# Front pooling in two-tile jobs, one per step, with the turned rows copied by ScalarE

## The reference

```python
h = rms_norm(x, norm1_g) * (1 + scale1) + shift1
z = h @ w_in                      # 256 columns p for pooling, then q, k, v of 6 heads
def pool_mixer(p, w_pool, pool_scale):       # windows 2, 4, 8, 16 tokens, one for each 64 channels
    pooled = stack([centred_mean(p_i, w) - p_i for each window w])
    return einsum('btgc,gcd->btgd', pooled, w_pool) * pool_scale
mix = concatenate([pool, attn]) @ w_out
```

## Time and profile before

| | us |
|---|---|
| median of 3 runs | 3398.87 (3396.64 to 3400.84) |
| the profiled execution, its own time | 3397.15 |
| its span, first to last instruction | 3395.4 |
| TensorE busy in the span | 3183.7 |
| VectorE busy | 2274.7 |
| ScalarE busy | 1610.0 |
| GpSimd busy | 631.9 |
| mean granted TensorE clock, share of full speed | 0.976 |

### The profile page before, as it was taken

The page is one execution under the profiler, slowest core; times in us unless marked ns, Lnnn a source line. Parts: engine busy times, 40 slices in busy tenths (PEclk is TensorE's granted clock), DMA queues, the critical chain, the costliest instruction groups (busy, mean ns, idle before and its releaser), DMA issues. The chain is left out here.

```text
span 3395.4 us, 69378 instructions
## 1 busy us (share of the span) xinstructions
PE 3183.7 (94%) x23534; PEld 2970.9 (87%) x23534; DVE 2274.7 (67%) x3793; ACT 1610.0 (47%) x3529; POOL 631.9 (19%) x854
## 2 busy tenths in 40 slices
PE   6879999999999999998987993999999999999998
PEld 4869988988998898997775882999999999999998
DVE  4778877877887887777884446555555555555553
ACT  3436656666665665665552110444444444444442
POOL 2432233232223223221000000000010010000001
PEclk8989999999999999999998995999999999999999
DMA  8554334334334335333326551665666666566663
GB/s 281 200 184 143 111 122 141 116 116 150 112 113 151 114 116 158 111 112 100 102 71 229 191 187 62 209 187 184 186 185 195 194 195 191 186 186 186 186 186 101
DMA packets 373718, 530.68 MB, mean 156 GB/s; under 512 B 29530, under 2 KB 321626, under 8 KB 358362
## 3 DMA queue, kind: packets, MB, share of 16 engines
q1 hardware_dynamic: 363868, 494.52, 44.8%
q0 software_dynamic: 9728, 34.61, 4.5%
HBM read 439.10 MB, written 89.16 MB: 156 GB/s over the span
## 5 line engine op out<-in xcount | busy, mean ns | idle before, releaser
L2421 PE MATMUL ps_gu<-xT,e_w 128*128 128x272 f32 x6144 | 788.1, 290 | 3.6 <-DVE xT L2596 3.6
L2421 PEld LDWEIGHTS ps_gu<-xT,e_w 128*128 128x128 f32 x6144 | 778.6, 189 | 4.2 <-issue 4.0
L2585 DVE TENSOR_TENSOR e_w<-e_raw,e_w 128x2048 fp32r<-128x2048 f32 x192 | 440.0, 2291 | 419.1 <-ACT e_w L2493 409.4
L1054 ACT ACTIVATE e<-ps_s,negm 128x1024 f32<-128x1024 f32 (+2 forms) x416 | 473.6, 1146 | 249.3 <-DVE negm L1387 249.3
L1379 DVE TENSOR_REDUCE mx<-ps_s 128x1 f32<-128x1024 f32 (+3 forms) x428 | 520.5, 1232 | 68.0 <-PE ps_s L722 67.3
L722 PE MATMUL ps_s<-kT,qT 128*128 128x512 f32 (+1 forms) x1920 | 469.5, 384 | 12.4 <-ACT e L1054 11.9
L760 PE MATMUL ps_m<-v,aT 128*128 128x128 f32 x3456 | 471.2, 279 | 6.6 <-ACT aT L1040 3.8
L760 PEld LDWEIGHTS ps_m<-v,aT 128*128 128x128 f32 x3456 | 420.7, 191 | 34.8 <-issue 14.8
L722 PEld LDWEIGHTS ps_s<-kT,qT 128*128 128x128 f32 x1920 | 346.8, 190 | 83.4 <-ACT e L1054 15.2
L2440 PE MATMUL ps_gu<-hid,e_w 128*128 128x272 f32 x3072 | 412.3, 291 | 0.0
L790 PE MATMUL ps_m<-w,hT 128*128 128x384 f32 x2040 | 391.9, 340 | 3.9 <-DVE o L1435 3.9
(11 more groups left out here) (287 smaller groups left out, 3273.9 us busy)
## 6 DMA issues: line engine op xcount, KB each, us to landing
hT<-hT_d SPq DMA_DIRECT2D x85, 1024.0 KB, 5.3
e_raw<-w_gate SPq DMA_DIRECT2D x64, 1024.0 KB, 5.0
e_raw<-w_up SPq DMA_DIRECT2D x64, 1024.0 KB, 5.0
e_raw<-w_down SPq DMA_DIRECT2D x64, 1024.0 KB, 7.6
tab<-tabs_d SPq DMA_DIRECT2D x85, 256.0 KB, 2.7
hT_d<-hT SPq DMA_DIRECT2D x17, 1024.0 KB, 4.0
cat_o<-cat_d SPq DMA_DIRECT2D x17, 1024.0 KB, 6.2
w_lent<-w_ada SPq DMA_DIRECT2D x16, 1024.0 KB, 5.4
```

Source lines behind the costliest of these rows:

```text
L1054: nc.scalar.activation(out, src, ACT.Exp, bias=negm[:, s.par, c:c + 1], scale=HD ** -0.5, accum_out=acc).then_inc(exp_done.sem, 1)
L2421: mm = nc.tensor.matmul(ps_gu[:, 2 * (s % 2) + f, 0:SLOTS], w_view(s, a)[:, k, f * P:f * P + P], xT[:, b, k, :], start=(k == 0 and a + b = ...
L2585: nc.vector.tensor_tensor(w[:, s % RING, 1, :], raw[:, s % RAW, :], w[:, s % RING, 0, :].bitcast(F32), ALU.subtract).then_inc(w_lo, 1)
```

## The change

- Pooling jobs have two tiles and one half each: 16 jobs, and two for the prompt (`JOBS` = 18). From step 3 on, `pool_sums` of one job ends VectorE's step; its mix, high and low parts follow in the next step; its save is issued in the step after. Jobs 14 to 17 (`LATE` = 14) have `pool_sums` at the end of step 16 and in the first step of head 1, where the remaining mixes are.
- Early jobs take two pooled buffers, two halves of the space of `aT` and two halves of one PSUM bank in turn; late jobs have places of their own in the half of `kT` that head 1 fills later. The buffers pT, trig and junk move to other places, and window sums use two buffers, not three.
- The copies of turned q, k and pooling rows go from VectorE's step to ScalarE's next step, behind `squares_kq` and ahead of `high_rows`.
- `spread_prompt` runs twice each in steps 0 and 1.
- Waits for the saves are added in head 1: `copy_turned`, `copy_past`, and VectorE's `copy_kq`.

```diff
+    JOBS, LATE, SPAN = NS + 2, NS - 2, 2 * P + 2 * PAD
...
+cat_early = aT[:].rearrange("p a n -> p (a n)").rearrange("p (q t l n) -> p q t l n", q=2, t=2, l=2)
+late_at = kT_lent[:, 2 * KEYS:4 * KEYS]
+pooled_early = e_lent[:, 0:512].rearrange("p (q n) -> p q n", q=2)
...
 def mixed_at(n):
-    return ps_t[:, 1, :] if n >= 6 and n % 2 else ps_m[:]
+    nt = pool_job(n)[2]
+    return ps_m[:, 2 * P * (n % 2):2 * P * (n % 2) + nt * P]
...
@@ SP, first_pass(t), after save_q and ahead of save_rows @@
-        for n in jobs_of(t - 1):
-            save_pooled(n)
+        if t >= 5:
+            save_pooled(t - 5)
...
@@ SP, body, ahead of the loads @@
         if s.h == 1 and s.zero:
-            for n in range(6, 10):
+            for n in range(NT - 5, LATE + 2):
                 save_pooled(n)
...
@@ SP, body, after save_q @@
+        if s.h == 1 and s.zero:
+            for n in range(LATE + 2, JOBS):
+                save_pooled(n)
...
@@ TensorE, mix_pool @@
+        if n:
             pe.wait_ge(catp_hi, n)
             pe.wait_ge(catp_lo, n)
...
@@ TensorE, first_pass, between turn_rows and project_pool @@
-        if 1 <= s.i <= 4:
-            spread_prompt(s.i - 1)
-        for n in jobs_of(s.i):
-            mix_pool(n)
+        if s.i < 2:
+            spread_prompt(2 * s.i)
+        if s.i >= 4:
+            mix_pool(s.i - 4)
...
@@ after project @@
+        if s.i < 2:
+            spread_prompt(2 * s.i + 1)
+        if s.i == NS:
+            mix_pool(LATE - 1)
...
@@ TensorE, body: mix_pool(LATE) ahead of scores(s, 0); ahead of scores(s, 1): @@
         if s.h == 1 and s.zero:
-            for n in (8, 9):
+            for n in range(LATE + 1, JOBS):
                 mix_pool(n)
-            pe.wait_ge(catp_hi, 10)
-            pe.wait_ge(catp_lo, 10)
...
@@ ScalarE @@
     def high_pooled(n):
-        if n == 9:
-            act.wait_ge(cat_b_saved, 16)
-        elif n and not in_cat_b(n):
-            act.wait_ge(cat_a_saved, 16 * cat_a_uses(n))
+        if 2 <= n < LATE:
+            act.wait_ge(pool_saved[n % 2], 16 * (n // 2))
...
+    def copy_kq(s):
+        kq_ready.wait(act, s, 1)
+        qT_saved[s.par].wait(act, s)
+        nc.scalar.copy(qT_out[:, s.par, :], ps_t[:, 1, 0:2 * P]).then_inc(kq_copied.sem, 1)
+        nc.scalar.copy(kT[:, 0, :, PAST + P * (s.i - 1):PAST + P * s.i],
+                       ps_t[:, 1, 2 * P:4 * P].rearrange("p (c n) -> p c n", c=2)).then_inc(kq_copied.sem, 1)
...
@@ ScalarE, first_pass, between squares_kq and high_rows @@
+        if s.i:
+            copy_turned_rows(previous(s))
...
@@ then, ahead of copy_pool @@
+        if s.i >= 4:
+            high_pooled(s.i - 4)
...
@@ ScalarE, body: copy_turned_rows first, high_pooled(LATE) ahead of split_rest(1), after exps(s, 0): @@
+        if s.h == 1 and s.zero:
+            for n in range(LATE + 1, JOBS):
+                high_pooled(n)
...
@@ VectorE, first_pass, from means to its end @@
-        for n in jobs_of(t):
-            low_pooled(n)
-        for n in jobs_of(t + 1):
-            pool_sums(n)
-        if t == NS:
-            pool_sums(6)
-            pool_sums(7)
+        if t >= 4:
+            low_pooled(t - 4)
         make_tab(s)
...
-        if s.kq:
-            copy_kq(s)
-        copy_pT(s)
+        if t >= 3:
+            pool_sums(t - 3)
+        if t == NS:
+            low_pooled(LATE - 1)
+            pool_sums(LATE)
+            pool_sums(LATE + 1)
...
@@ VectorE, body, ahead of maximum(s, 0, 0) @@
         if s.h == 1 and s.zero:
-            for n in (6, 7):
-                low_pooled(n)
-            for n in (8, 9):
+            low_pooled(LATE)
+            for n in range(LATE + 2, JOBS):
                 pool_sums(n)
-            for n in (8, 9):
-                low_pooled(n)
...
@@ VectorE, body, after negate(s, 0) @@
         if s.h == 1 and s.zero:
             split_rest(1)
+            for n in range(LATE + 1, JOBS):
+                low_pooled(n)
```

## The result

The changed kernel takes 3378.86 us (median of 4 runs, 3377.59 to 3379.48), the kernel before beside it 3397.76 (4 runs, 3394.53 to 3400.84): a ratio of 0.9948, 95% interval [0.9936, 0.9959], 18.9 us less. The forecast was 3382.6, its range 3375 to 3391. The profiled execution has a span of 3375.9 us in a time of 3377.59; before, 3395.4 in 3397.15.

The account below looks back on a forecast made before the run. TensorE, busy 94% of the span, was taken as the bound, so only its waits counted. 18.5 us from eleven steps, less 1.4 early and 0.8 at the border, made 16.3: from 3398.87 to 3382.6 us, range 3375 to 3391.

Parts of the forecast that it names:

- The wait for the save: First pass: two buffers in turn remove ScalarE's 28.3 us, in three waits, for the DMA that saves pooled rows.
- The loop: First pass, chain from project_pool through ScalarE and VectorE to the next: 8.44 us even, 9.36 odd; 9.7 odd with GpSimd.
- TensorE's own pace: First pass: 8.92 us plus half of a 512-column mix's 0.43, so 9.15 a step, binding even steps.
- GpSimd beside VectorE: First pass: GpSimd's low_kq and rsqrt_rows fall on make_tab and the first add; one add slowed, 0.35 us, was taken.
- Rival (b): First pass: VectorE and GpSimd slow each other every step, 9.2 and 10.3 us, total 3386.5; chance 0.20 (full slowing 3394, 0.05).
- The copies: First pass: three VectorE copies per tile, 0.415 us each, 21 us in all, go to ScalarE, costed at nothing there.
- The start: First two steps: job 0 and the prompt's row spreads, all moved there, cost about 0.2 us more.
- Job 1's step: Step from 89.17 to 98.06: 8.89 us without pooling, 10.1 with an odd job and edge products, a loss of 1.2.
- The border: Head 1's first step: scores' second half at E + 21.5 (E: last projection's end) for E + 20.7, 0.8 us lost.
- the signs that were named: First pass: no cat_d wait, steps of 9.2 and 9.7, clock 1.00, idle before odd mixes; head 1's scores at E + 21.5.
- Rival (a): First pass and border: GpSimd costs nothing, border neutral, eleven steps at 9.15, 20.5 us gained, 3378.4; chance 0.18.

Follow-up runs that it names:

- after: The changed kernel itself, with all edits of the change made to the kernel before: 3378.86 us, ratio 0.9948.
- The build-up: Five kernels adding parts of the change to the kernel before; first, an own buffer for jobs 1, 3 and 4: 3385.28 us, ratio 0.9973.
- the table's move: Changed kernel with VectorE making the rope table ahead of its wait for the means: 3375.52 us, ratio 0.9939.
- the kernel with 4-tile jobs: Kernel before plus own buffer for jobs 1, 3 and 4, copies on ScalarE and early spreads, without two-tile jobs: 3380.78 us, ratio 0.9952.
- both experiments: Spreads put into steps 0 and 1 on the kernel before, span 3395.1; one each in steps 0 to 3 on the changed kernel, span 3379.0.
- The experiment at the border: Changed kernel with the prompt jobs' high parts ahead of ScalarE's exponentials and VectorE's low parts around its maxima: 3372.97 us, ratio 0.9934.

## Why the prediction was right, and where it was not

**The wait for the save** goes, as forecast; its row is gone in after, and it comes back as 29.0 us with one buffer. The build-up shows its worth: 12.4 us of the eleven steps and 9.5 of the time, half of the gain, with the lower clock level that it brought.

**The loop.** Forecast: 103.2 us for eleven steps, 9.7 for an odd job and 9.2 for an even one. Measured: 101.04, with 9.73 and 9.00. The odd step was right, and the table's move showed that it is this loop. Two terms were off. The even steps were summed at 9.2 for 9.00. TensorE's own pace was read from a step of 8.92, and that step wasn't clean, since it still began behind a stall (clock 0.96, project_pool at 3.47 us for 3.12); a clean one takes 8.57, 0.35 less. The other half of the term erred the other way: the mix of two tiles was put at 0.22, half of 9.35 less 8.92, and costs 0.43 (9.00 less 8.57). Two errors met there, and what is left is six steps times 0.2, 1.2 us. And the interval from tile 15 to tile 16 took 8.12, where 9.2 was summed: step 16 has no rows to turn. That is 1.1 us, a step counted like the others without a look at what it issues.

**GpSimd beside VectorE.** One slowed add, 0.35 us, was the term taken. In the odd step it is the table: 1.30 us for two where 0.76 was the quick pair, while low_kq took 0.85 for 0.74; in the next, even step the table is quick and the first add takes 0.98 for 0.43. So 0.54 us a step, and in even steps under TensorE's pace, where it costs nothing. Rival (b) falls: 9.2 and 10.3 were not reached. (Its sum counts five odd steps, where the prediction had reasoned four of eleven; with four it is 105.6 us and not 106.7, which changes nothing here.) The Trainium skill (SBUF — State Buffer, Who interferes with whom) has a Vector instruction with two SBUF inputs and a GpSimd one that reads SBUF exclude each other, the later one waiting. These rows agree in that a pair grows by 0.54 us beside a GpSimd instruction of 0.74, which grows by 0.11; which of the two waited, they don't show.

**The copies.** Costed at nothing on ScalarE: right. Three of them stand in 0.79 us there (106.32 to 107.11 in after), less than the 0.35 to 0.69 each of the prediction, so ScalarE's busy time rose by 7.6 us, to 58.59 of 101.04, and not by 12 to 23; its longest waits are for TensorE and GpSimd. What their leaving is worth on VectorE was not priced alone. In the eleven steps it is 5.0 us with the save's wait in place, 5.8 with that gone, and 4.6 with one job per step. The times give nothing (0.9999), 2 us (0.9973 to 0.9967) and 9 (3388.1 against 3378.9), with intervals of 3 to 5 us each way that just meet, so that the worth depends on the save's wait is not shown.

The rule that the prediction weighed, that of the Trainium skill (VectorE: DVE Perf Modes, Rules for kernel authors) to keep chained Vector instructions few, spoke against the split. VectorE's busy time in the eleven steps is 85.21 us for 79.19 in the kernel with 4-tile jobs, so the split costs 6.0 there. The price was 1.8 for each four tiles, and three of the four groups fall into this window: 5.5, which is near. The whole kernels are equal in time, so here the rule's cost was real and was made up for elsewhere, by mixes that no longer wait.

**The start** was forecast as 0.2 us lost, and gained 2.0 (2.12 less 0.15). The step that failed is "moved into the first two steps, cost about 0.2 more": it priced what the spreads would cost where they go, and nothing for where they leave. The intervals from tile 2 and 3 alone gave 0.85 + 0.54 = 1.39, and both experiments point to the spreads' place: put early on before, they take 0.85 and 0.80 from these two, and in after 0.26 of the second goes to the mix of job 0. Of the other 0.6, in the intervals ahead of them, a part is left without a shown cause, and it is of the size by which the first tile's start varies.

**Job 1's step**: 1.2 us lost, 1.18 measured.

**The border** was forecast as 0.8 us lost, range 1.5 better to 4 worse; it lost 2.98 on the scores' second half, 2.37 on the next scores. The order was read rightly, and the lengths in VectorE's chain too, but it started late: pool_sums(13) ran beside GpSimd, so that the mix of job 13 came at E + 1.16, and low_pooled(13) started at E + 2.44 where it was to be over by E + 1.6. By the start of low_pooled(15), at E + 20.9 (226.46) for 19.5, that was 1.4 us. And from there low_pooled(15) and the two prompt jobs, one after the other on TensorE, ScalarE and VectorE, took 2.75 us to the scores (226.46 to 229.21) where 2.0 was summed: 0.75 more. The experiment at the border shows that this order was a choice and not a need.

So the sum was 16.3 us, the measured 19.5 of span: 2.2 more at the start, 2.2 more in the eleven steps, 2.2 less at the border, and about 1.1 behind it that was not in the sum. The total lay near because errors of both signs met, not because each term held: that the forecast is 3.7 us off, and not 6, is in part luck.

Of the signs that were named, the missing wait, the steps in turn, the clock, the idle time before the odd mixes and the wait for `ss` came as written. The scores didn't restart at E + 21.5, and one sign of being wrong came true: the border is longer than 23 us (23.67). Rival (a) has the nearer total, 3378.4, and nearly the measured eleven steps (100.7). Its mechanism is not the measured one: GpSimd does cost 0.54 us in the odd steps, these are 0.7 longer than the even ones, and the border is not neutral; that its number fits is luck too.

## What to carry to other kernels

Price a moved instruction at both its places: what it costs in the step that it leaves can be the larger number. Before splitting jobs, take away the waits around them one by one, since here a second buffer, copies on another engine and four spreads placed earlier took the same time without the split as with it. When several jobs are queued ahead of something that the critical engine needs, write down their whole chain over three engines, once for each job, and see first whether a part of it can stand ahead of the work that it waits behind. And where a part is worth no more than the spread of the times, read it from the window of the steps that it touches too: the copies' move shows nothing in the time and 5 us there.

## What the runs showed of the hardware

A total of DMA waits has no one price. In the kernel before, 28.3 us in three waits cost 12.4 us of the eleven steps. With one buffer in after, 22.7 us in twelve waits cost 3.3, and one of 6.3 at the border came with 5.1. The lower clock is in the price of the long ones: behind the first stall of before TensorE's clock was granted at 0.50, the 1.2 GHz level, and a turn of q and k took 1.08 us and a turn of rows 1.91, elsewhere 0.60 to 0.63 and 1.04.

```profile
131.70:134.63 2.93, 2.87 (x14) 2.90 (x15) 2.33 (x6) 1.15 (x7) 1.67 (x2) 0.50 0.42 121
```

A mix or a spread costs more than its own place. Those of 512 columns set project_pool back by 0.53 us and it runs 3.43 for 3.12; the 2-tile mix, of half the columns, costs 0.43 in all (9.00 less 8.57). A 4-tile mix costs 0.84 to 0.88 over its two intervals (9.10 to 9.14 and 8.88, each less 8.57), so twice the 2-tile one is the 4-tile one, and on TensorE the split is free. Why the instructions behind it are slower, no run here tells.
